# Sparse attention of a transformer block: the product of probabilities and values, in plain float32 or in three passes of rounded parts

## The reference

```python
logits = jnp.einsum('bthd,btkd->bhtk', qb, kg).astype(jnp.float32) * attn_scale
logits = logits + jnp.moveaxis(bias, -1, 1).astype(jnp.float32)
logits = jnp.where(valid[:, None], logits, -jnp.inf)
p = jax.nn.softmax(logits, axis=-1).astype(vg.dtype)
return jnp.einsum('bhtk,btkd->bthd', p, vg)
```

## Time and profile before

| | |
|---|---|
| time, median of 3 runs | 3156.46 us (3155.86 to 3160.37) |
| the profiled execution's own time | 3156.1 us |
| its span in the trace | 3154.2 us |
| TensorE busy | 2991.5 us, 95% |
| VectorE busy | 1988.7 us, 63% |
| ScalarE busy | 1235.4 us, 39% |
| GpSimd busy | 1613.9 us, 51% |
| attention stage, first to last line 1341 | 494.4 to 677.2 us |

### The profile page before, as it was taken

How to read it: one execution, slowest core, us unless ns; L and a number is a source line. 1 busy time by engine, 2 the same in 40 slices (tenths; PEclk the granted TensorE clock), 3 DMA queues, 4 the chain that set the end, 5 groups by cost and what they waited for, 6 DMA issues and landing times.

```text
span 3154.2 us, 39639 instructions
## 1 busy us (share of the span) xinstructions
PE 2991.5 (95%) x13018; PEld 2333.0 (74%) x13018; DVE 1988.7 (63%) x2941; ACT 1235.4 (39%) x1969; POOL 1613.9 (51%) x1022
## 2 busy tenths in 40 slices
PE   8999998999998999999899799989999899999998
PEld 6788785668876678888787576668666778877886
DVE  3899965546354677777548621255885676666648
ACT  3322214530334544444222332245675466662221
POOL 3254333324441378888679233284001477777877
PEclk9999998999999999999999899999999999999999
DMA  3122410025110244444984122442422257779774
GB/s 123 34 87 93 151 50 14 1 75 210 55 67 14 92 152 160 163 162 166 344 291 152 43 80 100 148 149 70 107 82 84 94 216 257 266 299 372 256 253 177
DMA packets 156892, 450.31 MB, mean 143 GB/s; under 512 B 17116, under 2 KB 28548, under 8 KB 156008
## 3 DMA queue, kind: packets, MB, share of 16 engines
q1 hardware_dynamic: 128944, 370.73, 33.7%
q10 hardware_dynamic: 27832, 78.08, 6.6%
HBM read 299.30 MB, written 148.13 MB: 142 GB/s over the span
## 4 chain that ended last, share of the span: by engine, by line
PE 69%; issue 9%; POOL 9%; DVE 8%; ACT 3%; DMA 1%; SPq 0%; POOLq 0%; ACTq 0%; DVEq 0%
PE ps L1118 19%; PE ps L1120 18%; PE ps L1119 18%; POOL left_lo L830 5%; PE ps L1168 3%; POOL part_in L825 2%; PE ps L1341 2%; PE ps L1720 1%; PE ps L1708 1%; PE ps L1331 1%; DVE sums_t L3150 1%; PE ps L1693 1%; PE ps L1694 1%; PE ps L1142 1%; DMA part_in<-mlp_weights_dram 1%
## 5 line engine op out<-in xcount | busy, mean ns | idle before, releaser
L830 POOL TENSOR_TENSOR left_lo<-part_in,left_hi 128x512 fp32r<-128x512 f32 x414 | 572.5, 1396 | 252.8 <-ACT left_hi L2562 93.0
L725 POOL TENSOR_TENSOR w_hi<-w_raw,zero 128x1024 fp32r<-128x1024 f32 x71 | 138.1, 1945 | 514.1 <-PE ps L1120 508.0
L825 POOL TENSOR_TENSOR part_in<-part_in,part_in 128x512 f32<-128x512 f32 x252 | 361.1, 1433 | 36.9 <-DMA part_in<-mlp_weights_dram 16.1
L1118 PE MATMUL ps<-h_hi,w_hi 128*128 128x512 f32 x528 | 206.6, 391 | 1.4 <-ACT wi_t L1934 1.4
L1119 PE MATMUL ps<-h_lo,w_hi 128*128 128x512 f32 x528 | 205.8, 390 | 0.0
L1120 PE MATMUL ps<-h_hi,w_lo 128*128 128x512 f32 x528 | 205.7, 390 | 0.0
L728 POOL TENSOR_TENSOR w_lo<-w_raw,w_hi 128x1024 fp32r<-128x1024 f32 x71 | 188.5, 2655 | 5.6
L751 POOL TENSOR_TENSOR w_hi<-w_raw,zero 128x512 fp32r<-128x512 f32 x5 | 8.3, 1659 | 350.5 <-PE ps L1120 350.5
L1118 PE MATMUL ps<-down_t,left_hi 128*128 128x512 f32 x432 | 169.6, 393 | 5.2 <-POOL left_lo L830 2.8
L1120 PE MATMUL ps<-down_t,left_lo 128*128 128x512 f32 x432 | 168.4, 390 | 0.0
L1119 PE MATMUL ps<-down_t,left_hi 128*128 128x512 f32 x432 | 168.4, 390 | 0.0
(11 more groups left out here) (575 smaller groups left out, 8693.8 us busy)
## 6 DMA issues: line engine op xcount, KB each, us to landing
w_raw<-weights_dram SPq DMA_DIRECT2D x102, 512.0 KB, 3.2
part_in<-ffn_weights_dram SPq DMA_DIRECT2D x144, 256.0 KB, 3.2
part_in<-mlp_weights_dram SPq DMA_DIRECT2D x144, 256.0 KB, 4.6
mlp_parts_scratch<-part_t SPq DMA_DIRECT2D x64, 512.0 KB, 4.6
down_t<-mlp_parts_scratch SPq DMA_DIRECT2D x64, 512.0 KB, 6.5
ffn_parts_scratch<-part_t SPq DMA_DIRECT2D x44, 512.0 KB, 4.6
down_t<-ffn_parts_scratch SPq DMA_DIRECT2D x44, 512.0 KB, 6.3
mlp_parts_scratch<-part_b SPq DMA_DIRECT2D x32, 512.0 KB, 5.0
```

The source lines that it names most:

```text
L725: nc.gpsimd.tensor_tensor(w_hi[s][:], raw[s][:], zero[:, 0:1].broadcast_to([P, 1024]), ALU.add).then_inc(w_rounded, 1)
L825: tt(part_in[p][dst][:], part_in[p][dst][:], part_in[p][other][:], ALU.add).then_inc(left_summed, 1)
L830: tt(lo[:], src[:], hi[:].bitcast(F32), ALU.subtract).then_inc(w_split, 1)
L1118: nc.tensor.matmul(out, sh, mh, start=start, stop=False)
```

## The change

The values are kept as a pair: ScalarE copies them to the high part as before (now rounded to fp32r), and VectorE subtracts it from PSUM to make the low part. The same is done for every transposed tile of probabilities: ScalarE's copy becomes the rounding of the high part, and VectorE makes the low part at the end of its step. TensorE makes the product in the three passes of `product`. It waits for VectorE's count `probs_rest` where it waited for `pt_out`, in the product and before the reuse of a PSUM bank by a transposition. `probs_rest` is the semaphore `guard_ready`, used a second time, so the two later waits for the latter count from `guard_0`, which is 72.

```diff
-        value = at("value", BR + 32 * KB, [P, NT, P])
+        value = pair("value", BR + 32 * KB, [P, NT, P])
...
-        probs_t = [at(f"probs_t{i}", BR + 40 * KB + 2 * KB * i, [P, HALF]) for i in range(2)]
+        probs_t = [pair(f"probs_t{i}", BR + 40 * KB + 4 * KB * i, [P, HALF]) for i in range(2)]
...
+        probs_rest, guard_0 = guard_ready, tiles_before(2 * NT)
...
-            pool.wait_ge(guard_ready, 1)
+            pool.wait_ge(guard_ready, guard_0 + 1)
...
             pe.wait_ge(pooled_ready, POOL_GROUPS)
-            pe.wait_ge(value_out, 1)
+            pe.wait_ge(value_out, 2)
...
             pe.wait_ge(masks_ready, 1)
-            pe.wait_ge(value_out, 1)
+            pe.wait_ge(value_out, 2)
...
                 if n_tr >= 2:
-                    pe.wait_ge(pt_out, n_tr - 1)
+                    pe.wait_ge(probs_rest, n_tr - 1)
...
-                pe.wait_ge(pt_out, n_tr + 1)
-
-                nc.tensor.matmul(ps[:, 6 + group % 2, :], value[:, j, :], probs_t[n_tr % 2][:], start=j == 0,
-                                 stop=j == group // 2).then_inc(pv_done, 1)
+                pe.wait_ge(probs_rest, n_tr + 1)
+                product(ps[:, 6 + group % 2, :], tuple(v[:, j, :] for v in value), tuple(v[:] for v in probs_t[n_tr % 2]),
+                        j == 0, j == group // 2).then_inc(pv_done, 1)
...
-            nc.scalar.activation(value[:], wide(2).rearrange("p (j n) -> p j n", j=NT), ACT.Copy).then_inc(value_out, 1)
+            nc.scalar.activation(value[0][:], wide(2).rearrange("p (j n) -> p j n", j=NT), ACT.Copy).then_inc(value_out, 1)
...
-                        nc.scalar.activation(probs_t[n_tr % 2][:], ps[:, 4 + n_tr % 2, :], ACT.Copy).then_inc(pt_out, 1)
+                        nc.scalar.activation(probs_t[n_tr % 2][0][:], ps[:, 4 + n_tr % 2, :], ACT.Copy).then_inc(pt_out, 1)
...
             in_lo(3, [part[:] for part in key], wide(0))
+            dve.wait_ge(value_out, 1)
+            tt(value[1][:], wide(2).rearrange("p (j n) -> p j n", j=NT), value[0][:].bitcast(F32), ALU.subtract).then_inc(value_out, 1)
...
                     if n == 1 and group + 2 < 2 * NT:
                         rest_query(group + 2)
+                    for j in tiles_of(group, n):
+                        n_tr = tiles_before(group) + j
+                        hi, lo = probs_t[n_tr % 2]
+                        dve.wait_ge(pt_out, n_tr + 1)
+                        tt(lo[:], ps[:, 4 + n_tr % 2, :], hi[:].bitcast(F32), ALU.subtract).then_inc(probs_rest, 1)
             mix_out_lo(2 * NT - 1)
...
-            dve.wait_ge(guard_ready, 1)
+            dve.wait_ge(guard_ready, guard_0 + 1)
```

## The result

The changed kernel takes 3203.32 us (median of 4 runs, 3201.78 to 3205.79) against 3157.47 for the kernel before timed beside it: a ratio of 1.0145, 95% interval 1.0127 to 1.0162. It is slower by 45.9 us; 39.6 were forecast.

The account below looks back on a forecast made before the run. TensorE's stream was taken as the bound, lengthened by waits for VectorE's late subtraction: 33.6 us over the groups plus 6 for clock falls, 39.6 on 3156.1, gives 3196 us; forecast 3184 to 3208 (67%), range 3170 to 3222.

Parts of the forecast that it names:

- What decides: Whether VectorE, working in program order, makes the low part in time for TensorE's next values product; not its busy share.
- The schedule of group 6: Step-by-step timing of this four-head group, one tile per step, at full clock: from 9.7 to 14.2 us, +4.5.
- group 4: Four-head group with three tiles: 11.85 us at full clock, entered in the sum as +2.0.
- step 1: Second of a group's four steps, subtraction behind the query's low part; new waits of 2.2 to 2.6 us, groups 4 to 13.
- The clock: TensorE falling to half clock behind new waits: half of nine falls at 1.4 us, 6 us; bounds 0 and 13.
- The gain of the passes: Values product on TensorE: three passes 0.69 us against 0.86, 0.17 a tile, 12 us over 72 tiles without new waits.
- Group 14: Late group with no query left to split, only its last step waits: +0.7 us net.
- The signs in the trace: Expected in the changed trace: subtraction waits 25 to 35 us, given group lengths, same time outside 490 to 715 us.
- That the subtraction hides: Rival: VectorE finishes the low part within the next logits, so TensorE gives back 12 us: 3144; chance 5%.
- That only the one-tile groups lose: Rival: groups 10 to 15 absorb waits and gain 7 us, groups 0 to 9 lose 22.8: 3172; chance 13%.
- That the clock stays low: Rival: TensorE at 1.2 GHz through groups 4 to 13, 32 us on top of 33.6: 3222; chance 12%.
- Costs at nothing: Values' low-part subtraction before key selection, hidden by later VectorE idling; 1.2 us if that cover were gone.

Follow-up runs that it names:

- low_first: Changed kernel with VectorE's probabilities subtraction moved ahead of the unit's inverse and the queries' low part; 3170.33 us, ratio 1.0034 to the kernel before.
- plain_waits: Changed kernel with the plain float32 product, the probabilities' subtraction still made and waited for, its result unused, the values' subtraction left out; 3214.25 us, ratio 1.0179.
- no_low: Changed kernel without the probabilities' subtraction: three passes with the high part twice, waiting only for ScalarE's copy; 3150.11 us, ratio 0.9971 to the kernel before.
- filled: Changed kernel with seven extra unread 512-column matmuls on TensorE ahead of the values products of two steps per group; 3198.50 us, ratio 1.0126 to the kernel before.
- start_filled: Kernel before the change with unread matmuls filling TensorE's idle time at the head of the stage; 3157.53 us, ratio 1.0006.
- two_passes: Changed kernel without the probabilities' subtraction and third pass: rounded probabilities times the values' high and low parts; 3140.44 us, ratio 0.9949 to the kernel before.

## Why the prediction was right

- **What decides: right.** The sum rested on VectorE's program order, not on its share of busy time. low_first moves 35 of 46 us with the same instructions, and plain_waits has all of the loss without the passes. The traces of the stage put sizes to it: the passes alone give 5.9 us (186.0 to 180.1, no_low), the subtraction ahead of the inverse and the queries costs 15.9 (to 196.0, low_first), and its place at the end of the step 39.1 (to 235.1), the falls of the clock included.
- **The schedule of group 6 and of the others: right.** In groups that kept the clock the measured lengths are the forecast ones: group 4 11.85 us (11.85), group 7 14.9 (14.5), group 11 17.4 (16.7). The distance of 4.60 us in step 1 stands against 4.65. In filled, groups 6 to 13 take 132.7 us where the schedule has 129.7, each 0.2 to 0.7 more. One entry of the sum is wrong: group 4 at 11.85 is 1.5 above its 10.4, not 2.0.
- **The clock: price right, number of falls too small.** The prediction took half of nine falls, 6 us. There were eight between 545 and 713 us, each 3.4 us long and each worth about 1.4 us, so 11 us. The groups they touch (5, 6, 8, 9, 10, 12, 13, 14) are 1.3 to 2.1 us longer than scheduled, together 13 us, of which 2 to 3 are the drift that filled shows without a fall. Seven came in the step-1 waits, or at most 1.2 us behind their end; these waits are 1.9 to 2.3 us long. The eighth came at the wait of 3.45 us ahead of group 15. The count was a guess between bounds and the bounds held. The same waits in groups 4, 7 and 11 (2.43, 2.06 and 1.91 us) had no fall, so a wait of this length makes one likely here and no more; which of them the clock follows is not shown. Half was too few, by 5 us. Group 2, at 0.50 for most of its length because the clock came back at 515 us and not at 504, adds 1.7 us that no term had.
- **How near the sum came: in part luck.** The stage grew by 49.1 us, 9.5 more than the 39.6, which was meant for it alone. The rest of the trace was 2 us shorter, and the medians differ by 1.4 us less than the two traces; so 45.9 is nearer than the stage was.
- **The gain of the passes: right sign, too large.** 12 us added up, 9 measured (no_low, 5 to 13); in the full stream of its trace a tile gives 0.125 us and not 0.17.
- **Group 14: wrong by 1.6 us.** +0.7 was forecast, +2.3 measured. The fall of the clock in it would account for 1.4 of the 1.6.
- **The signs in the trace.** Group 6 near 14 us (15.5), group 12 near 18 (20.1), group 14 nearly unchanged (it was not), waits of 25 to 35 us for the subtraction (49.2: the forecast counted what the stage loses; the waits also hold the time that the passes save and old waits that went) with a longest of 2 to 2.6 in step 1 (2.43 there, and the 3.45 ahead of group 15, which had not been foreseen), nothing outside the stage (2 us less).
- **The rivals.** That the subtraction hides fell with the result and with plain_waits. That only the one-tile groups lose: with the order as changed groups 10 to 14 lose 17.7 us, so it fell too, but it describes low_first, where groups 12 to 14 gain 2.4 us and the early ones lose. That the clock stays low fell for groups 4 to 13: it came back after 3.4 us each time. Only at the head of the stage did it stay low longer than before (to 515 us).
- **Costs at nothing.** The stage starts at 492.8 us in place of 492.6. The values' low part is hidden.

## What to carry to other kernels

An operation put between two engines costs by its place in its engine's program, not by the engine's free share: look what it stands behind, and whether that thing waits for a third engine. When a step is made longer by a chain, shorter matmuls in it are worth their time only on the chain; and a chain that leaves TensorE idle for some 2 us in every round can cost clock on top. Here it did in seven rounds of ten, at 1.4 us each; such a term is better given with its bounds than halved.

## What was not expected of the hardware

Seven extra matmuls in each of two waits a group made the stage 8.4 us shorter (235.1 to 226.7): in groups 5 to 13 the granted clock stayed at 1.00 (2.4 GHz) where it had fallen seven times to 0.50 (1.2 GHz), and passes stayed 0.23 us apart in place of 0.42.

The length of a wait did not tell whether the clock falls: behind the 1.97 us at the start of group 4 it fell in the kernel before and not in start_filled; a wait of 2.43 us (group 4, changed kernel) had no fall, and one of 1.43 us (ahead of group 15, two_passes) had one.
